# Moving a row scaling, table arithmetic, identity turns and activation-table loads in a whole-model kernel

## The chip, the cores and the metric

One core of a Trainium2 chip runs the whole program. The metric is the device time of one execution in microseconds (us); lower is better. The core has a matrix engine (PE), a vector engine (DVE), an activation engine (ACT), GpSimd (POOL) and a sync engine (SP) that issues transfers; each runs its own queue in order, and they meet only at semaphores.

## The reference

Two small networks run one after the other over 256 tokens of width 1024. The first also carries 256 context tokens. Its two layers are each a mixer (a gated delta rule, then attention), followed by an expert layer that picks 16 of 16384 experts per head and token. The second has two layers, each with a mixer, a feed-forward part with a causal convolution, and a gated embedding. What matters here:

```
def rmsnorm(x, gain):
    y = xf * lax.rsqrt(jnp.mean(xf * xf, axis=-1, keepdims=True) + EPS)
    return (y * gain).astype(x.dtype)

# the expert layer, per block of 128 tokens
    top_s, top_i = lax.top_k(s, PEER_TOPK)                 # 16 of 128, twice per head
    cand_s = top_s[..., 0, :, None] + top_s[..., 1, None, :]
    best_s, pos = lax.top_k(cand_s, PEER_TOPK)             # 16 of 256
    gate = jax.nn.softmax(best_s, axis=-1)
    act = jax.nn.gelu(jnp.einsum('pd,phkd->phk', xb, u_tab[idx]))
    return jnp.einsum('phk,phkd->pd', gate * act, v_tab[idx])

def conv_ffn(x, w_up, conv_w, conv_b, w_down):
    h = x @ w_up                                           # 1024 -> 5632
    hc = conv_b + sum(conv_w[j] * shifted(h, j) for j in range(3))
    g, up = jnp.split(hc, 2, axis=-1)
    return (jax.nn.silu(g) * up) @ w_down                  # 2816 -> 1024
```

The mixer of the second network's second layer is a state-space scan. It needs tables of powers of complex numbers (`Er`, `Ei`), which depend on weights alone and can be worked out at any time before it.

## The kernel before

The program is a list of stages (Begin, Ada, DeltaNet, Peer a, Attention, Peer m, FinalNorm, EvenMixer, Ffn 0, Ple 0, S5, Ffn 1, Ple 1, End). In a stage every engine has a hand-written order (`pe`, `dve`, `act`, `pool`, `sp`). Before its work in a stage an engine runs `enter`, which waits for all engines of the stage before; so no engine starts a stage until the last one has left the one before. Weights go through a ring of three 1 MB buffers that SP fills as PE frees them.

**Norms.** 128 tokens make a tile. ACT squares and sums one tile of a pair, DVE the other; DVE forms the mean, ACT takes the root (`Sqrt`, L340, L1618 or L2348), DVE inverts it (`reciprocal`) and scales the rows (`dve_scale`). PE turns the scaled tile in blocks of 128x128 into PSUM, and ACT and DVE each apply gain and shift to half of it while they copy it to `hT`. ACT evaluates functions from a table that must be loaded; the compiler puts a table load ahead of the first instruction that needs another one, so the one for the root stands between the squares and the root. While the first scaled tile is on its way, PE turns the identity 24 times into a bank that nobody reads (`pe_busy`, `BUSY = 24`). In the DeltaNet stage the first tile has already been scaled in the stage before.

**Expert stages (`Peer`).** Peer a has four tiles and 32 units (tile by head), Peer m two tiles and 16 units. For each unit `dve_choose` picks 16 experts: a generator with 14 steps, one or more DVE instructions each. POOL then gathers 16 rows of 8 KB per token, in 16 indirect transfers, into eight slots; DVE forms 16 dot products (`dve_dot`, L1993), ACT the gelu and a diagonal matrix, PE the weighted sum (L1858). A slot is filled again when PE has used it. The norm's scratch lies in the last two slots, so gather 6 waits until the last tile has passed the norm (`pool_rows`). Ahead of the sums, PE forms the queries and scores of eight half heads in pairs, jobs 0 to 7 (L1816, L1829): jobs 0 to 3, then the turns of tiles 2, 3 and 4, then jobs 4 to 7, for which all tiles must be in `hT`. The scaled rows have two buffers; in Peer a the fourth tile (number 3) needs the buffer of the second. DVE works through choice 0, choice 1, the scaling of tile 3, and then the units, with a step of the choice for the unit after next behind every dot product.

**Ffn 0.** The up projection is 44 chunks of 128 features (PE L300, four PSUM banks). For each chunk DVE does three instructions of the convolution (L2863, L2865, L2867) and, from chunk 22 on, a multiplication by the gate (L2872). Behind every chunk from the third on it also does two steps of the tables for the state-space mixer (L2745 to L2768); `pieces(c)` gives the number. The down projection (PE L262) starts when DVE has done chunk 43; DVE then adds its four results to the residual (L2879). Ffn 1 is the same without table steps.

Of the kernel before, what the change touches and what calls it, by code (L numbers as in the profile page):

```python
# [12 lines left out]
ACT = mybir.ActivationFunctionType  # L13
# [103 lines left out]
class Kit:  # L117


    def __init__(self, nc, ins, out, ctx):  # L120
# [13 lines left out]
        self.arena = self.tensor("arena", self.arena_n)  # L134
        self.top, self.rings = 0, [self.ring]

    def count(self, name, step=1):
# [7 lines left out]
    def tensor(self, name, n, dt=F32):  # L145
        return self.ctx.enter_context(self.nc.sbuf_tensor(name, [128, n], dt))[:, :]

    def al(self, n):
# [24 lines left out]
class Stage:  # L173
# [22 lines left out]
    def pe(self, e):  # L196
        pass
# [4 lines left out]
    def act(self, e):  # L202
        pass
# [105 lines left out]
class Norm:  # L309
# [88 lines left out]

    def pe(self, e):
        st = self.st  # L400
        self.pe_busy(e)
        for n in range(len(self.tiles)):
            e.wait_ge(*st.V.at(("n_x", n)))
            for half in range(2):
                if n >= 2:
                    e.wait_ge(*(st.V if half else st.S).at(("nT", n - 2)))
                for c in range(4):
                    m = st.turn(e, st.k.banks[(2 * n + half) % 4][:, c * 128:(c + 1) * 128],
                                self.xn[n % 2][:, (half * 4 + c) * 128:(half * 4 + c + 1) * 128])
                m.then_inc(*st.P.up(("nt", n, half)))  # L410
# [53 lines left out]
class Begin(Stage):  # L464
# [6 lines left out]
    def pool(self, e):  # L471
        k, i = self.k, self.k.i
        e.dma_start(k.cv, i["consts"][:, 0:k.nconst]).then_inc(*self.lc.up("c"))
        for name, d in (("ctx", 0), ("x", 2)):
            e.dma_start(k.X[:, d:d + 2, :], i[name][0].rearrange("(t p) d -> p t d", p=128)).then_inc(*self.lx.up())
# [108 lines left out]
class DeltaNet(Stage):  # L584
# [153 lines left out]
    def pe(self, e):  # L738
        k, P, ring = self.k, self.P, self.k.ring
        self.enter(e)  # L740
        self.norm.pe(e)
        e.wait_ge(*self.l_cw.at("l"))
# [941 lines left out]
class Peer(Stage):  # L1684
# [179 lines left out]
    def act(self, e):  # L1864
        k, P, V, S = self.k, self.P, self.V, self.S
        self.enter(e)
        self.norm.act_first(e)
# [12 lines left out]
        for u in range(self.units):  # L1880
            steps = self.act_steps(u)
# [72 lines left out]
    def dve(self, e):  # L1954
# [6 lines left out]
        for _ in self.dve_choose(e, 0):  # L1961
            pass
        for u in range(self.units):
            t = u // 8
            if u == 0:
                steps = itertools.chain(self.dve_choose(e, 1), self.dve_choose(e, 2))
                for _ in range(14):
                    next(steps)
                if self.nt > 2:
                    self.norm.dve_scale(e, 3)  # L1970
            else:
                steps = self.dve_choose(e, u + 2) if u + 2 < self.units else iter(())
# [9 lines left out]
            if u % 8 == 2 and u > 8:  # L1982
                self.dve_add(e, t - 1)
        self.dve_add(e, self.nt - 1)

    def dve_dot(self, e, u, s):
# [186 lines left out]
class Attention(Stage):  # L2173
# [76 lines left out]

    def act(self, e):
        self.enter(e)
        S = self.S
# [75 lines left out]
class FinalNorm(Stage):  # L2329
# [8 lines left out]

    def act(self, e):
        self.enter(e)  # L2340
        S = self.S
# [22 lines left out]
class EvenMixer(Stage):  # L2364
# [110 lines left out]

    def act(self, e):
        self.enter(e)
        S, V = self.S, self.V
# [293 lines left out]
class Ffn(Stage):  # L2772
# [35 lines left out]
    def pieces(self, c):  # L2808
        return 0 if self.l or c < 3 else 2

# [24 lines left out]
    def act(self, e):  # L2835
        k, V, S = self.k, self.V, self.S
        self.enter(e)
        self.norm.act(e)
# [11 lines left out]
    def dve(self, e):  # L2850
# [7 lines left out]
        for c in range(44):  # L2858
# [14 lines left out]
            for _ in range(self.pieces(c)):  # L2873
                next(steps, None)
        for n0 in (0, 512):
            for t in range(2):
# [5 lines left out]
class Ple(Stage):  # L2882
# [34 lines left out]
    def act(self, e):  # L2917
        S = self.S
        self.enter(e)
        self.norm.act(e)  # L2920
# [27 lines left out]
class S5(Stage):  # L2948
# [83 lines left out]
    def act(self, e):  # L3032
        V, S = self.V, self.S
        self.enter(e)
        self.norm.act(e)
# [178 lines left out]
```

## Time and profile before

| | |
|---|---|
| median of 3 runs | 4298.86 us (4298.03 to 4300.78) |
| profiled execution, its own time | 4287.95 us |
| its span in the trace | 4286.2 us |
| busy: PE, DVE, ACT, POOL | 85%, 59%, 23%, 28% |
| granted PE clock, mean | 0.966 of full |
| moved by the transfers | 1043.68 MB, mean 244 GB/s |

The span is the profiled execution from its first to its last instruction; the 1.75 us between it and the execution's own time lie around it. Stages in the trace, in us from the span's start: the first norm 36 to 48, the DeltaNet stage to 1115, Peer a 1115 to 2493, Attention to 2642, Peer m to 3350, Ffn 0 3517 to 3783, S5 from 3824, Ffn 1 4000 to 4240. A busy share is an average over all of them and says little of one place; what a change is worth there is read from the wait that ends last there.

### The profile page before, as it was taken

The numbers are of one execution on the slowest core, as the hardware profiler recorded it, in microseconds if no ns is written. First come the engines' busy times: TensorE is split into PE (matmuls) and PEld (weight loads), VectorE is DVE, ScalarE is ACT, GpSimd is POOL, SyncE is SP. The second block draws the span as 40 slices with busy tenths as digits, with TensorE's granted clock in tenths as the row PEclk, the third lists the DMA queues.
The fourth block names the chain that finished last, engine by engine and source line by source line (L and its number), as shares of the span: only waits on it lengthen the run. The fifth ranks groups of instructions, "written<-read, shape, count | busy, mean of one in ns | idle before, by whom it ended". The sixth has DMA issues, their size and how long they took to land.

```text
span 4286.2 us, 59878 instructions
## 1 busy us (share of the span) xinstructions
PE 3650.8 (85%) x23128; PEld 1996.2 (47%) x23128; DVE 2514.1 (59%) x5831; ACT 966.8 (23%) x2602; POOL 1219.4 (28%) x1257
## 2 busy tenths in 40 slices
PE   7988899888899977776777789887777889899999
PEld 3467544675444432222232236443222368555774
DVE  3466435564566777776777655667776348535341
ACT  2333113331222222222222213222222121010100
POOL 1054000440134444444444400344444010015000
PEclk9999999899999999999999999999999999999999
DMA  8200244001599999999999933999999334330443
GB/s 291 83 4 4 89 158 158 4 4 50 201 384 404 410 419 420 418 415 412 411 413 416 413 123 121 412 416 418 412 414 415 134 93 138 123 103 20 143 146 127
DMA packets 270115, 1043.68 MB, mean 244 GB/s; under 512 B 19931, under 2 KB 104166, under 8 KB 171530
## 3 DMA queue, kind: packets, MB, share of 16 engines
q0 software_dynamic: 115184, 815.62, 46.7%
q1 hardware_dynamic: 154650, 224.23, 15.5%
q8 instruction: 187, 3.06, 0.3%
q14 instruction: 94, 0.77, 0.1%
HBM read 1038.64 MB, written 1.13 MB: 243 GB/s over the span
## 4 chain that ended last, share of the span: by engine, by line
PE 52%; DMA 25%; DVE 12%; ACT 4%; issue 4%; POOL 3%; SPq 0%; DVEq 0%; POOLq 0%; ACTq 0%
DMA arena<-in_peer_uv,arena 25%; PE psum L262 13%; PE psum L1858 12%; PE psum L772 5%; PE psum L300 5%; PE psum L1816 4%; PE psum L816 3%; DVE arena L1993 2%; PE psum L213 2%; PE psum L1162 1%; POOL arena L1951 1%; PE psum L508 1%; ACT arena L1893 1%; PE psum L1173 1%; POOL arena L3055 1%
## 5 line engine op out<-in xcount | busy, mean ns | idle before, releaser
L1858 PE MATMUL psum<-arena 128*128 128x512 f32 x3072 | 1458.9, 620 | 394.1 <-ACT arena L1893 389.3
L1993 DVE SCALAR_TENSOR_TENSOR arena<-arena 128x1024 bf16<-128x1024 f32 x768 | 941.0, 1225 | 523.6 <-DMA arena<-in_peer_uv,arena 492.1
L1951 POOL DMA_INDIRECT arena<-in_peer_uv,arena x768 | 855.4, 1114 | 1184.8 <-PE psum L1858 1055.2
L1858 PEld LDWEIGHTS psum<-arena 128*128 128x128 f32 x3072 | 573.8, 195 | 1227.8 <-ACT arena L1893 634.6
L262 PE MATMUL psum<-ring,arena 128*128 128x512 f32 (+1 forms) x1344 | 576.4, 590 | 24.6 <-DVE arena L2872 9.1
L262 PEld LDWEIGHTS psum<-ring,arena 128*128 128x128 f32 x1344 | 254.2, 192 | 340.3 <-issue 315.1
L1886 ACT ACTIVATE arena<-arena 128x2 f32<-128x2 f32 x384 | 78.2, 204 | 1242.7 <-DVE arena L1993 1242.7
L1893 ACT ACTIVATE arena<-consts,arena 128x128 f32<-128x128 f32 x768 | 268.4, 394 | 224.0 <-DVE arena L2005 221.5
L300 PE MATMUL psum<-arena,ring 128*128 128x256 f32 x1408 | 309.6, 381 | 9.8 <-DVE arena L2867 7.7
L300 PEld LDWEIGHTS psum<-arena,ring 128*128 128x128 f32 x1408 | 267.0, 191 | 50.4 <-issue 6.4
L772 PE MATMUL psum<-arena,ring 128*128 128x512 f32 x512 | 229.0, 600 | 1.6 <-issue 1.6
L1816 PE MATMUL psum<-arena,ring 128*128 128x128 f32 (+3 forms) x704 | 183.0, 411 | 8.9 <-ACT arena L1631 8.9
L1816 PEld LDWEIGHTS psum<-arena,ring 128*128 128x128 f32 x704 | 120.7, 200 | 79.1 <-issue 50.8
L772 PEld LDWEIGHTS psum<-arena,ring 128*128 128x128 f32 x512 | 95.4, 191 | 127.4 <-issue 121.5
L213 PE MATMUL psum<-consts,arena 128*128 128x128 f32 (+3 forms) x706 | 102.9, 287 | 55.5 <-DVE arena L1672 12.3
L3055 POOL TENSOR_TENSOR arena<-arena 128x512 f32<-128x512 f32 x32 | 40.6, 1269 | 331.1 <-DVE arena L3090 331.1
L213 PEld LDWEIGHTS psum<-consts,arena 128*128 128x128 f32 (+3 forms) x706 | 84.0, 147 | 103.9 <-issue 44.6
L816 PE MATMUL psum<-ring,arena 128*128 128x512 f32 x256 | 110.4, 593 | 1.6 <-ACT arena L951 1.6
L2005 DVE SCALAR_TENSOR_TENSOR arena<-arena 128x2 f32<-128x2 f32 x384 | 80.9, 211 | 33.1 <-ACT arena L1886 31.4
L1014 DVE SCALAR_TENSOR_TENSOR arena<-arena 128x512 f32<-128x512 f32 x128 | 96.2, 752 | 4.5
L2863 DVE TENSOR_SCALAR arena<-psum,arena 128x256 f32<-128x256 f32 x88 | 47.6, 541 | 84.9 <-PE psum L300 84.7
L2879 DVE TENSOR_TENSOR x_res<-x_res,psum 128x512 f32<-128x512 f32 x8 | 5.5, 687 | 152.4 <-PE psum L262 152.4
(412 smaller groups left out, 3894.9 us busy)
## 6 DMA issues: line engine op xcount, KB each, us to landing
arena<-in_ada_w SPq DMA_DIRECT2D x48, 1024.0 KB, 7.1
ring<-in_ffn_w_up SPq DMA_DIRECT2D x44, 1024.0 KB, 5.0
ring<-in_dn_w_in SPq DMA_DIRECT2D x24, 1024.0 KB, 5.6
ring<-in_peer_w_query SPq DMA_DIRECT2D x22, 1024.0 KB, 7.0
ring<-in_ffn_w_down SPq DMA_DIRECT2D x20, 1024.0 KB, 5.0
arena<-in_peer_uv,arena POOLq DMA_INDIRECT x768, 12.8
ring<-in_ev_w_in SPq DMA_DIRECT2D x10, 1024.0 KB, 5.1
ring<-in_dn_w_out SPq DMA_DIRECT2D x8, 1024.0 KB, 4.8
```

The costliest lines, as they stand in the source:

```text
L213: return e.transpose(out, in_, self.k.const("ident")[0:n, 0:n])
L262: m = e.matmul(o, self.hT[:, k0 + k, t * 128:(t + 1) * 128], w[:, k, :], start=k0 + k == 0, stop=k0 + k == self.KC - 1)
L300: m = e.matmul(self.bank(c)[:, 0:self.nt], w[:, k, j * 128:(j + 1) * 128], self.hT[:, k, 0:self.nt], start=k == 0, stop=k == self.KC - 1)
L772: m = e.matmul(self.job_bank(j), w[:, q, j % 2 * 128:(j % 2 + 1) * 128], self.hT[:, q, :], start=q == 0, stop=q == 7)
L816: m = e.matmul(k.banks[t * 2 + nh], self.oT[:, k0 + q, t * 128:(t + 1) * 128], w[:, q, nh * 512:(nh + 1) * 512], start=k0 + q == 0, stop=k ...
L1014: e.scalar_tensor_tensor(acc, p[:, :, w:w + 256], self.cw[:, c, w:w + 1], acc, MUL, ADD).then_inc(*V.up(("conv", half, j)))
L1816: m = e.matmul(k.banks[j % 2][:, 0:w_], w[:, n, c % 2 * 128:(c % 2 + 1) * 128], self.hT[:, n, a * 128:b * 128], start=n == 0, stop=n == 7)
L1858: m = e.matmul(k.banks[4 + t % 2 * 2 + nh], self.diag[g % self.ND], self.vsl[g % self.NS][:, nh * 512:(nh + 1) * 512], start=u % 8 == 0 an ...
L1893: e.activation(self.diag[g % self.ND], k.const("ident"), ACT.Copy, bias=0.0, scale=self.cf[u % 2][:, s:s + 1]).then_inc(*S.up(("dg", g)))
L1951: e.indirect_dma_start(self.uv[g % self.NS], None, self.table(), bass.IndirectOffsetOnAxis(ap=self.eid[u % 6][:, s:s + 1], axis=0)).then_i ...
L1993: e.scalar_tensor_tensor(self.junk[g % 2], self.us[g % self.NS], 1.0, self.h[:, u // 8, :], MUL, MUL, accum_out=self.a[u % 2][:, s:s + 1]) ...
L3055: e.tensor_tensor(self.xr[i % 8], self.w2[i % 4], self.two(T.Er[:, i, :]), MUL).then_inc(*G.up())
```

## The change

- The 24 identity turns are left out in the norm of the DeltaNet stage; the other norms keep them.
- `root_table` is called first thing by ACT in ten stages, ahead of `enter`: a `Sqrt` of one column that POOL has set to 1 at the start of the program. The table load moves to it.
- In Peer a DVE scales tile 3 between choice 0 and choice 1.
- In both expert stages choice 2 starts behind the third dot product of unit 0 and not behind the first (`late`).
- In Ffn 0 DVE does two table steps behind chunks 3 to 21 and one behind chunks 22 to 43, and the rest behind chunk 43, while PE is in the down projection.

```diff
+    def root_table(self, e):
+        e.activation(self.warm[1], self.warm[0], ACT.Sqrt, bias=0.0, scale=1.0)
...
-    def pe(self, e):
+    def pe(self, e, busy=True):
         st = self.st
-        self.pe_busy(e)
+        if busy:
+            self.pe_busy(e)
...
     def pool(self, e):
         k, i = self.k, self.k.i
+        e.memset(k.warm[0], 1.0).then_inc(*self.G.up())
...
-        self.norm.pe(e)
+        self.norm.pe(e, busy=False)
...
     def act(self, e):
         k, P, V, S = self.k, self.P, self.V, self.S
+        k.root_table(e)
         self.enter(e)
...
         for _ in self.dve_choose(e, 0):
             pass
+        if self.nt > 2:
+            self.norm.dve_scale(e, 3)
+        for _ in self.dve_choose(e, 1):
+            pass
         for u in range(self.units):
             t = u // 8
             if u == 0:
-                steps = itertools.chain(self.dve_choose(e, 1), self.dve_choose(e, 2))
-                for _ in range(14):
-                    next(steps)
-                if self.nt > 2:
-                    self.norm.dve_scale(e, 3)
+                steps = self.late(self.dve_choose(e, 2), 2)
...
+    def late(self, steps, n):
+        for _ in range(n):
+            yield
+        yield from steps
...
     def pieces(self, c):
-        return 0 if self.l or c < 3 else 2
+        return 0 if self.l or c < 3 else 2 if c < 22 else 1
...
+        for _ in steps:
+            pass
         for n0 in (0, 512):
```

**Order of DVE in Peer a, where choice 0 ends.** The 128x16 SCALAR_TENSOR_TENSOR ends a choice, `x_res,arena 128x1024` is the scaling of a tile, and 128x1024 SCALAR_TENSOR_TENSOR a dot product. Before (the rest of choice 1 is left out):

```order
L2073 SCALAR_TENSOR_TENSOR arena<-arena 128x16
L2024 MAX arena<-arena 128x8
...
L2073 SCALAR_TENSOR_TENSOR arena<-arena 128x16
L1672 TENSOR_SCALAR arena<-x_res,arena 128x1024
L1993 SCALAR_TENSOR_TENSOR arena<-arena 128x1024
L2024 MAX arena<-arena 128x8
L2026 MAX_INDEX arena<-arena 128x8
L1993 SCALAR_TENSOR_TENSOR arena<-arena 128x1024
L2028 MATCH_REPLACE arena<-arena 128x128
L2030 MAX arena<-arena 128x8
L2002 RECIPROCAL arena<-arena 128x1
```

The same place in the changed kernel:

```order
L2087 SCALAR_TENSOR_TENSOR arena<-arena 128x16
L1679 TENSOR_SCALAR arena<-x_res,arena 128x1024
L2038 MAX arena<-arena 128x8
...
L2087 SCALAR_TENSOR_TENSOR arena<-arena 128x16
L2007 SCALAR_TENSOR_TENSOR arena<-arena 128x1024 x2
L2016 RECIPROCAL arena<-arena 128x1
L2019 SCALAR_TENSOR_TENSOR arena<-arena 128x2
L2007 SCALAR_TENSOR_TENSOR arena<-arena 128x1024
L2038 MAX arena<-arena 128x8
L2040 MAX_INDEX arena<-arena 128x8
```

The scaling has moved ahead of choice 1, and the first steps of choice 2 behind the third dot product.

**Order of DVE in Ffn 0, at its end.** The first four rows of a chunk are the convolution and the gate (128x256 to 128x254), 128x1016 and 128x8x127 are table steps, `x_res` is the residual. Before:

```order
L2872 TENSOR_TENSOR arena<-arena 128x256
L2764 TENSOR_TENSOR arena<-arena 128x1016
L2768 TENSOR_TENSOR arena<-arena 128x8x127
L2863 TENSOR_SCALAR arena<-psum,arena 128x256
L2865 SCALAR_TENSOR_TENSOR arena<-psum,arena 128x255
L2867 SCALAR_TENSOR_TENSOR arena<-psum,arena 128x254
L2872 TENSOR_TENSOR arena<-arena 128x256
...
L2879 TENSOR_TENSOR x_res<-x_res,psum 128x512 x4
```

In the changed kernel:

```order
L2785 TENSOR_TENSOR arena<-arena 128x8x127
L2882 TENSOR_SCALAR arena<-psum,arena 128x256
L2884 SCALAR_TENSOR_TENSOR arena<-psum,arena 128x255
L2886 SCALAR_TENSOR_TENSOR arena<-psum,arena 128x254
L2891 TENSOR_TENSOR arena<-arena 128x256
L2778 TENSOR_TENSOR arena<-arena 128x1016
L2781 TENSOR_TENSOR arena<-arena 128x1016
L2785 TENSOR_TENSOR arena<-arena 128x8x127
...
L2900 TENSOR_TENSOR x_res<-x_res,psum 128x512 x4
```

Fifteen table steps now stand behind the last chunk and ahead of the four additions.

**Order of ACT where Ffn 0 begins.** `x_res 128x1024` is the square, 128x2 the root. Before:

```order
L451 ACTIVATE arena<-psum 128x4x128 x2
L335 ACTIVATE arena<-x_res 128x1024
L340 ACT_TABLE_LOAD
L340 ACTIVATE arena<-arena 128x2
L348 ACTIVATE arena<-psum,vc 128x128 x8
```

In the changed kernel:

```order
L457 ACTIVATE arena<-psum 128x4x128 x2
L151 ACT_TABLE_LOAD
L151 ACTIVATE warm<-warm 128x1
L340 ACTIVATE arena<-x_res 128x1024
L345 ACTIVATE arena<-arena 128x2
L353 ACTIVATE arena<-psum,vc 128x128 x8
```

The load has moved ahead of the wait for the stage before and of the square; there are as many loads as before. On PE the only difference is that the one row of 24 identity turns ahead of DeltaNet's first tile is gone; SP's order is the same.

## Rows read from the trace of the kernel before

**Rows 1.** The page, chain that ended last: share of the span by engine.
```profile
PE 52%; DMA 25%; DVE 12%; ACT 4%; issue 4%; POOL 3%; SPq 0%; DVEq 0%; POOLq 0%; ACTq 0%
```

**Rows 2.** Timeline, first norm: start, length, engine, line, operation, out<-in [idle before <-releaser].
```profile
36.15 4.48 PE L213 MATMUL psum<-consts 128*128 128x128 f32 x24 [0.81 <-PE psum L562]
...
38.54 0.60 POOL L722 DMA_DIRECT2D arena<-in_dn_conv_w  x1
...
41.54 1.36 DVE L385 TENSOR_SCALAR arena<-psum,mod 128x128 f32<-128x128 f32 x4 [3.85 <-PE psum L213]
...
48.16 3.65 PE L754 MATMUL psum<-arena,ring 128*64 128x512 f32 x16 [1.08 <-ACT arena L348]
```

**Rows 3.** One line's answer, L722: its transfer.
```profile
DMA to landing us min/median/max: 5.6/5.6/5.6
```

**Rows 4.** Windows, first norm: length, busy PE, PEld, DVE, ACT, POOL, clock, DMA, GB/s.
```profile
36.15:40.40 4.25, 4.25 (x24) 4.25 (x25) 1.54 (x1) 0.00 (x0) 3.95 (x8) 0.60 1.05 384
...
40.40:48.10 7.70, 4.58 (x40) 3.83 (x37) 6.56 (x19) 6.24 (x17) 4.25 (x8) 1.00 1.05 350
```

**Rows 5.** Timeline, first expert stage, before its sums.
```profile
1134.07 5.68 ACT L1631 ACTIVATE arena<-psum,mod 128x128 f32<-128x128 f32 x16
...
1136.03 0.17 DVE L2073 SCALAR_TENSOR_TENSOR arena<-arena 128x16 uint32<-128x16 f32 x1
...
1145.55 0.74 DVE L1672 TENSOR_SCALAR arena<-x_res,arena 128x1024 f32<-128x1024 f32 x1
...
1147.57 2.90 ACT L1631 ACTIVATE arena<-psum,mod 128x128 f32<-128x128 f32 x8 [7.81 <-PE psum L213]
...
1150.52 6.45 PE L1816 MATMUL psum<-arena,ring 128*128 128x128 f32 x32 [2.14 <-ACT arena L1631]
```

**Rows 6.** Windows, the same stage: cold stretch, first sums, later sums.
```profile
1146.40:1156.00 9.60, 7.42 (x33) 7.05 (x34) 1.03 (x2) 3.18 (x9) 1.89 (x2) 0.50 1.01 423
...
1167.00:1203.00 36.00, 36.00 (x94) 16.78 (x93) 24.49 (x64) 8.45 (x25) 13.65 (x12) 0.96 0.82 296
...
1500.00:1900.00 400.00, 306.79 (x651) 121.27 (x651) 296.34 (x747) 100.44 (x279) 174.98 (x160) 0.97 1.01 418
```

**Rows 7.** Timeline of DVE, feed-forward 0, two table steps in a chunk.
```profile
3616.84 0.54 DVE L2863 TENSOR_SCALAR arena<-psum,arena 128x256 f32<-128x256 f32 x1
...
3618.86 1.20 DVE L2764 TENSOR_TENSOR arena<-arena 128x1008 f32<-128x1008 f32 x1
...
3621.22 0.54 DVE L2863 TENSOR_SCALAR arena<-psum,arena 128x256 f32<-128x256 f32 x1
...
3742.49 0.69 DVE L2879 TENSOR_TENSOR x_res<-x_res,psum 128x512 f32<-128x512 f32 x1 [39.41 <-PE psum L262]
```

**Rows 8.** Timeline of PE, feed-forward 0.
```profile
3587.79 56.28 PE L300 MATMUL psum<-arena,ring 128*128 128x256 f32 x260
...
3644.49 3.69 PE L300 MATMUL psum<-arena,ring 128*128 128x256 f32 x16 [0.42 <-DVE arena L2867]
...
3703.18 7.09 PE L262 MATMUL psum<-ring,arena 128*128 128x512 f32 x9 [6.96 <-DVE arena L2872]
```

**Rows 9.** Timeline of PE, feed-forward 1, where the down projection starts.
```profile
4161.80 4.94 PE L262 MATMUL psum<-ring,arena 128*128 128x512 f32 x7 [2.18 <-DVE arena L2872]
```

**Rows 10.** Windows, start of both down projections.
```profile
3703.20:3709.20 6.00, 6.00 (x7) 2.48 (x8) 0.00 (x0) 0.00 (x0) 0.00 (x0) 0.50 0.00 0
...
4161.80:4166.60 4.80, 4.80 (x8) 2.02 (x9) 0.00 (x0) 0.00 (x0) 0.00 (x0) 0.64 0.46 180
```

**Rows 11.** Groups by line, table loads of L340: busy us, mean ns, idle.
```profile
L340 ACT ACT_TABLE_LOAD x7 | 9.0, 1283 | 0.1
```

**Rows 12.** Timelines of three norms: first turns on data.
```profile
2498.44 1.97 PE L213 MATMUL psum<-consts,arena 128*128 128x128 f32 x16 [0.49 <-DVE arena L392]
...
3520.59 2.34 PE L213 MATMUL psum<-consts,arena 128*128 128x128 f32 x20 [0.88 <-DVE arena L392]
...
3828.78 1.91 PE L213 MATMUL psum<-consts,arena 128*128 128x128 f32 x16
```

More of the change, by code:

```diff
@@ L135, in __init__ @@
         self.top, self.rings = 0, [self.ring]
+        self.warm = [self.tensor(f"warm{n}", 1) for n in range(2)]
     def count(self, name, step=1):
@@ L2251, in act @@
     def act(self, e):
+        self.k.root_table(e)
         self.enter(e)
@@ L2339, in act @@
     def act(self, e):
+        self.k.root_table(e)
         self.enter(e)
@@ L2476, in act @@
     def act(self, e):
+        self.k.root_table(e)
         self.enter(e)
@@ L2836, in act @@
         k, V, S = self.k, self.V, self.S
+        k.root_table(e)
         self.enter(e)
@@ L2918, in act @@
         S = self.S
+        self.k.root_table(e)
         self.enter(e)
@@ L3033, in act @@
         V, S = self.V, self.S
+        self.k.root_table(e)
         self.enter(e)
```

## The prediction

> **What bounds the kernel now.** I read the page's chain first, then the chain in order of time, to find which stages are held by what; then the timeline at each place the change touches, and windows for clock and transfers. The chain is more than half PE, a quarter transfers and an eighth DVE [rows 1], but no edit touches the bulk of any of these: each sits at a seam, where one engine waits for another. The reader should look, at each seam, for the idle time ahead of the instruction that leads on. There are four kinds.
>
> In the first norm PE turns 24 identities, 4.48 us, while nobody else works, and only then the data on which DVE waits 3.85 us [rows 2]. In Peer a ACT is done with tiles 1 and 2 at 1139.75 and idles until tile 3 arrives at 1147.57, because DVE ran all of choice 1 ahead of that tile's scaling [rows 5]. In Ffn 0 PE gets through a chunk (16 matmuls) each 56.28 x 16 / 260 = 3.46 us until 3644, and is then held by DVE chunk for chunk [rows 8]; DVE takes 4.38 us for a chunk with two table steps [rows 7]. In the other norms PE waits for the scaled rows 0.49 or 0.88 us, or not at all [rows 12]. The measurement of this kernel can tell some 0.2%, 8.6 us, from no change.
>
> **Ffn 0, the largest term.** One table step is taken from each chunk from 22 on. A chunk's own work on DVE is 3618.86 - 3616.84 = 2.02 us, a step 1.20 [rows 7]: 3.22 per chunk, under PE's 3.46. PE finished chunk 31 at 3644.07 (the 56.28 us piece), so chunk 22 at 3644.07 - 9 x 3.46 = 3612.9; DVE came to it at 3616.84, 3.9 us late. It gains 0.24 per chunk, is level with PE near chunk 38, and meanwhile stays far inside the four banks. So PE is never held, and ends chunk 43 at 3644.07 + 12 x 3.46 = 3685.6. Ffn 1 is the model for what follows: there, without table steps, PE waits 2.18 us for the last chunk [rows 9]. The down projection then starts at 3687.8 and not at 3703.18 [rows 8]: 15.4 us. If DVE does not catch up (22 chunks of 3.3 from 3616.84) it is 13.8.
>
> The 15 steps left over, 15 x 1.20 = 18 us, are hidden by the down projection: the first addition to the residual comes 39.3 us after the projection starts [rows 7, 8]. Without that cover they would cost 18 us.
>
> The wait before the down projection also left PE at half clock: 0.50 over the first 6.00 us of it, which is 3.0 us lost; Ffn 1, after its short wait, ran 4.80 us at a mean of 0.64, so 72% of it at half, 1.7 lost [rows 10]. I take Ffn 1's case, 1.3 us more; at best 3.0. Term: **16.7 us**, 13.8 to 18.4.
>
> **Peer a, tile 3.** Choice 0 ends at 1136.2, and the buffer that the scaling needs is free (ACT already copies that tile from 1134.07). The scaling, 0.74, ends near 1137.0 and not at 1146.3. PE turns it at once, but ACT is on tiles 1 and 2 until 1139.75; then come its 2.90 us for tile 3, and jobs 4 to 7 can start at 1142.7 where they started at 1150.52 [rows 5]: 7.8 us. What is late next is ACT, not DVE: choice 1 ends 0.7 later, at 1146.2, while the first gelu needs jobs 4 to 7 to be done; two of them took 6.45 us [rows 5], so all four end near 1153. Gathers 6 and 7, behind the norm on POOL, move with it. Then the clock: PE ran at half from 1146.4 to 1156.0 [rows 6], so 5.5 us of these jobs, 2.7 lost. PE's idle time is now broken by the eight turns, so part of that may return; zero to 2.7, and I take 1.0, nearer to zero because the rest of the idle stretch remains. From the first sums on, everything hangs on the slots that PE frees; the transfers have room there (0.82 busy) and are full only later (1.01) [rows 6], so the whole full stretch starts earlier with the same bytes. Term: **8.8 us**, 7.8 to 10.5.
>
> **First norm.** The eight turns of tile 0 start at 36.15; at the pace of the identity turns, 4.48 / 24 = 0.187, they end at 37.65, and DVE's copy begins 3.9 us earlier than 41.54 [rows 2]. Not all of this arrives. The five turns of the convolution weights stand in PE's queue ahead of the gate matmuls, and these weights land at 38.54 + 5.6 = 44.1 whatever PE does [rows 2, 3]; with up to 0.9 for the turns, the matmuls start near 44.9 and not 48.16: 3.3 us. Against it stands the clock: over the identity turns it was 0.60 on average, and 1.00 over the stretch behind them [rows 4]. With the gaps that real turns have, the half level may last into the matmuls, and each us of it there costs 0.5. None gives 3.3; lasting to 50.5 gives 0.5. I take 2 us of it: **2.3 us**.
>
> The Trainium skill, TensorE: Matmul & The Clock Gate, part 4 (PE-mode transpose), says that turns do not count as PE activity as matmuls do and that the full clock does not engage for them. By that rule the 24 turns never raised the clock, leaving them out costs nothing, and this term would be 3.3, the sum 31.1. The trace disagrees: PE had nothing but these turns from 36.15, and the clock was full behind them [rows 4]. I go by the trace.
>
> **Square root's table.** A load is 1.28 us [rows 11] and stood behind the square. Where it moves ahead of `enter`, ACT was waiting for the stage before. What it frees is capped by PE's idle time before its first turns on data [rows 12]: 0.49 in Attention, 0.88 in Ffn 0 and (the same row) in Ffn 1. In S5 PE goes straight from the identity turns to the data, so nothing; the same holds in both expert stages, the two Ple stages load it while PE is in another projection, FinalNorm waits for its gain row, and EvenMixer has the table already. Behind these caps the identity turns are late next. Term: **2.3 us**; 1.5 if the small root itself delays `enter` where ACT had worked until just before.
>
> **Choice 2 later; POOL's memset.** Two of 14 choice steps move from a stretch in which DVE waits into the sums of unit 0. The nearest row for a step is the table step, 1.20, so at most 2.4 per stage if nothing hid it; but DVE is busy 24.49 of 36.00 us in the first sums [rows 6]. I take 0, bounds -0.5 to +1.2. The memset, one column ahead of the first loads on POOL, is 0 to 0.1.
>
> **Sum.** 16.7 + 8.8 + 2.3 + 2.3 = 30.1 us. Against the profiled execution's own 4287.95 (span 4286.2 and 1.75 around it) that is 4257.9. This execution was 10.9 faster than the median of the runs shown, so for a median I predict 4298.86 - 30.1 = **4268.8 us**. With all low ends the gain is 22, with all high ends 35: 4264 to 4277.
>
> **Rivals.**
> - *The gathers swallow Peer a's gain.* For it: the transfers are full for most of the stage, and gathers 0 to 5 start no earlier. Against it: only eight slots exist, so the early start of six moves nothing behind them, and the transfers have room in the first sums. The gain would be 21.3: 4277.6.
> - *The table steps were not what held PE*, so Ffn 0 stays as it was and the change does not do there what it says. Against it: PE's waits name DVE's L2867 [rows 8], and Ffn 1, with the same loads and chunks, has none of them. The gain would be 13.4: 4285.5.
> - *Slower: PE stays at half clock without the identity turns*, through the gate matmuls and DeltaNet's first projections, which PE sets. Every us at half costs 0.5, so it decides from 60 us at half clock on. At 90 us it costs 45, and with the other terms kept the time is 4298.86 - 30.1 + 45 = 4313.8. For it: the half level lasted 9.6 us at one place with PE 77% busy [rows 6]. Against it: 90 us is nine times that, and these matmuls follow without gaps.
>
> **Chances.** Forecast 0.73, gathers 0.12, Ffn 0 unchanged 0.06, half clock 0.04, and 0.05 for small terms adding up beyond the high end. The range reaches from a little under the high end, for the spread between executions (the profiled one and the median are 10.9 apart), to past the first rival: 4257 to 4281; the forecast alone 4264 to 4277. Faster by over 0.2% holds for the forecast, the first rival, two thirds of the second and what lies beyond the high end: 0.94. Within 0.2% are the rest of the second, where another term fails too, and a mild half clock: 0.03. Slower: 0.03.
>
> **What would show it.** In the changed profile, Ffn 0: no idle PE between chunks, about 2.2 us of it before the down projection, and 15 table steps beside that. Peer a: jobs 4 to 7 start about 3 us after ACT is through with tile 2, not 10.8. First norm: the gate matmuls start about 8.8 us after the first turn of the stage, not 12.0. Norms of Ffn 0 and 1: no PE idle before the turns. It is wrong if in Ffn 0 the down projection starts over 50 us after chunk 32 (before 58.7, forecast 43.3), or if Peer a from its first sum to its last grows by what its start gained.

## Result and the profile after the change

| | before | after |
|---|---|---|
| median of the runs, us | 4298.44 (4296.43 to 4300.78, 4 runs) | 4259.48 (4256.97 to 4262.81, 4 runs) |
| profiled execution, own time (span), us | 4287.95 (4286.2) | 4262.81 (4261.0) |
| mean granted clock | 0.966 | 0.969 |

The ratio is 0.991, 95% interval 0.9892 to 0.9927. The change makes the kernel faster by 39.0 us between medians; forecast were 30.1, a time of 4268.8 and a range of 4257 to 4281. The time lies in the range, but 4.5 us below the fast end of the forecast alone (4264 to 4277). The interval in us is 31 to 46. In a second measurement (e8 below) the gain was 35.9 us, interval 0.9904 to 0.9931, which is 29.6 to 41.2 us. So the gain is probably some us more than the sum of 30.1: the first interval excludes it, the second does not. The two profiled executions differ by only 25.1 us, because that of before was a quick one (4287.95, where 29 later runs of the same kernel had a median of 4294.77) and that of after was the slowest of its four.

The page of after, the chain that ended last by engine, answers to [rows 1]: DVE has lost 3 points of it.

```profile
PE 54%; DMA 26%; DVE 9%; ACT 4%; issue 3%; POOL 2%; DVEq 0%; POOLq 0%; ACTq 0%
```

**Ffn 0.** PE's timeline of after. The columns here and below: start, length, engine, line, operation, operands, count, and in brackets the idle time before it and who ended it.

```profile
3567.82 110.67 PE L305 MATMUL psum<-arena,ring 128*128 128x256 f32 x512
3680.67 9.68 PE L267 MATMUL psum<-ring,arena 128*128 128x512 f32 x22 [2.18 <-DVE arena L2891]
```

The 512 matmuls of the last 32 chunks are now one row without a wait: 110.67 / 32 = 3.46 us a chunk, the pace that the prediction took from [rows 8]. Chunk 32 starts at 3567.82 + 20 x 3.46 = 3637.0, so the down projection starts 43.7 us after it (before 58.7, forecast 43.3), behind the 2.18 us that [rows 9] had promised. DVE's timeline shows where the table steps went:

```profile
3680.60 1.22 DVE L2778 TENSOR_TENSOR arena<-arena 128x1016 f32<-128x1016 f32 x1
...
3697.49 1.22 DVE L2785 TENSOR_TENSOR arena<-arena 128x1016 f32<-128x1016 f32 x1
...
3716.99 0.69 DVE L2900 TENSOR_TENSOR x_res<-x_res,psum 128x512 f32<-128x512 f32 x1 [18.28 <-PE psum L267]
```

From 3680.60 to 3697.49 there are fifteen of them, all beside the down projection, and DVE then still waits 18.28 us for the first sum. Nothing of them is on the path.

**Peer a.** The timeline of the seam that [rows 5] shows for before:

```profile
1137.17 8.47 ACT L1638 ACTIVATE arena<-psum,mod 128x128 f32<-128x128 f32 x24
...
1139.22 0.74 DVE L1679 TENSOR_SCALAR arena<-x_res,arena 128x1024 f32<-128x1024 f32 x1
...
1140.11 1.97 PE L218 MATMUL psum<-consts,arena 128*128 128x128 f32 x8 [2.84 <-ACT arena L1638]
...
1145.69 5.91 PE L1823 MATMUL psum<-arena,ring 128*128 128x128 f32 x32 [3.62 <-ACT arena L1638]
```

ACT's idle time of 7.81 us is gone: its 16 copies for tiles 1 and 2 and the 8 for tile 3 are one row of 24. ACT is late next, as forecast. It is through with tile 2 after 16 / 24 of 8.47, at 1142.82, and jobs 4 to 7 start 2.9 us later (before 10.8, forecast 3). The window of 9.6 us from these jobs on, which answers to the first of [rows 6]:

```profile
1145.60:1155.20 9.60, 9.36 (x62) 9.17 (x63) 5.91 (x16) 1.38 (x6) 3.28 (x4) 0.77 1.00 414
```

The clock is 0.77 there, where it was 0.50.

**First norm.** Timeline of after, against [rows 2], and the windows against [rows 4] (length, busy PE, PEld, DVE, ACT, POOL, clock, DMA, GB/s):

```profile
37.06 3.41 PE L218 MATMUL psum<-consts,arena 128*128 128x128 f32 x16 [0.82 <-PE psum L569]
...
38.80 1.36 DVE L390 TENSOR_SCALAR arena<-psum,mod 128x128 f32<-128x128 f32 x4 [0.66 <-PE psum L218]
...
40.01 0.94 POOL L729 DMA_DIRECT2D arena<-in_dn_conv_w  x1
...
46.02 0.49 PE L218 MATMUL psum<-consts,arena 32*128 32x32 f32 x5 [2.11 <-DMA arena<-in_dn_conv_w]
...
46.44 5.35 PE L761 MATMUL psum<-arena,ring 128*64 128x512 f32 x16
```

```profile
40.40:46.40 6.00, 2.64 (x22) 2.10 (x21) 5.15 (x15) 5.06 (x12) 5.95 (x11) 0.97 1.06 357
46.40:51.80 5.40, 5.40 (x19) 1.54 (x18) 0.32 (x1) 0.23 (x1) 0.00 (x0) 0.68 0.36 121
```

The gate matmuls follow the stage's first turn by 9.4 us (before 12.0, forecast 8.8). PE was held by the convolution weights, as expected, which POOL issued 1.5 us later than in [rows 2]: 0.9 because the stage itself began later, and 0.5 because the second of the two memsets ahead of them took 1.07 us and not 0.53. It took about 1.07 in all the other traces with it ahead of the weights (e1 to e9, e11, e12), so this is not an effect of the change, and the trace of before was the lucky one. The start won 1.7 us, and the same 16 matmuls took 5.35 us at a clock of 0.68 where they had taken 3.65: 1.7 lost. The first projection begins at 51.72 (before 51.74). By these two traces alone, the first norm gave nothing.

**Norm of Ffn 0**, against [rows 12]: the turns on data follow the identity turns at once.

```profile
3510.78 2.81 PE L218 MATMUL psum<-consts 128*128 128x128 f32 x24 [0.83 <-PE psum L267]
3513.57 1.97 PE L218 MATMUL psum<-consts,arena 128*128 128x128 f32 x16
```

### The profile page after: what moved, and what is told of

It reads as the page before. It is cut to its first block, busy times and chain, and to the rows that moved or that the text cites. A ratio compares the mean times of both kernels' runs of the same rounds, so it can differ in the third digit from the quotient of the medians.

```text
span 4261.0 us, 59845 instructions
## 1 busy us (share of the span) xinstructions
PE 3639.4 (85%) x23104; PEld 1989.0 (47%) x23104; DVE 2517.2 (59%) x5831; ACT 968.8 (23%) x2612; POOL 1221.6 (29%) x1258
## 3 DMA queue, kind: packets, MB, share of 16 engines
q1 hardware_dynamic: 154650, 224.23, 15.7%
## 4 chain that ended last, share of the span: by engine, by line
PE 54%; DMA 26%; DVE 9%; ACT 4%; issue 3%; POOL 2%; DVEq 0%; POOLq 0%; ACTq 0%
DMA arena<-in_peer_uv,arena 26%; PE psum L267 13%; PE psum L1865 12%; PE psum L305 7%; PE psum L779 5%; PE psum L1823 3%; PE psum L823 3%; DVE arena L2007 2%; PE psum L218 2%; PE psum L1169 1%; ACT arena L1901 1%; PE psum L1180 1%; PE psum L515 1%; POOL arena L3078 1%; POOL arena L1959 1%
## 5 line engine op out<-in xcount | busy, mean ns | idle before, releaser
L1415 POOL COPY arena<-arena 32x128 f32<-32x128 f32 x128 | 38.1, 297 | 174.3 <-DVE arena L1540 166.3
```

## Experiments

Gains are given between medians against the kernel before on the same chip; an interval in us is that of the ratio times 4295. Since every kernel's trace has the same matmuls, identity turns apart, stretches between the starts of the same matmul can also be compared in 14 traces (before, after, e1 to e12), and the table below holds them. The stretch of Peer a starts at the turns of tile 2, 15.5 us into the stage in every trace; the last three rows start at the stage's first identity turn. E10 is not in the first row, since it has a second edit there. One trace stands for each kernel (two for the whole change). By "pattern of the clock" I mean at which seams the granted clock is full and at which it is half. Within one pattern the late stretches repeat within 0.2 us, which no run of the whole program does.

| stretch, by PE's starts | traces without the edit, us | traces with it, us | gain |
|---|---|---|---|
| first matmul to DeltaNet's second half | 514.3 to 517.7, mean 515.8 (9) | 511.0 to 514.0, mean 512.4 (4) | 3.4 |
| Peer a | 1358.8 to 1362.5, mean 1360.5 (8) | 1350.8 to 1353.5, mean 1352.1 (6) | 8.5 |
| Ffn 0 and Ple 0: table steps | 307.57 to 307.65 (5) | 290.77 (e1) | 16.8 |
| the same, root's table on top | 290.77 (e1) | 288.17 to 288.21 (5) | 2.6 |
| S5: root's table | 175.87 or 175.88 (6) | 174.39 to 174.41 (5), or 177.41 and 177.58 (2) | 1.5, or -1.6 |
| Ffn 1 and Ple 1: root's table | 278.67 or 278.68 (5) | 276.06 or 276.07 (4), or 277.50 to 277.55 (3) | 2.6, or 1.1 |

### e1: the table steps of Ffn 0 alone

```diff
-        return 0 if self.l or c < 3 else 2
+        return 0 if self.l or c < 3 else 2 if c < 22 else 1
...
+        for _ in steps:
+            pass
```

> Only Ffn 0's table steps are moved; everything else is as in the kernel before. My theory (DVE's second table step per chunk held PE from chunk 32 on): the down projection of Ffn 0 starts 43 to 45 us after chunk 32 (58.7 before), and the time falls by 16.7 us (13.8 to 18.4). Rival theory, that the 9 us by which the medians moved more than my sum sit here (the steps beside the down projection or the chunks gave more than counted): 22 us or more. Second rival, that the table steps did not hold PE: 0 to -2 us.

Measured: 4277.46 us, ratio 0.9965, interval 0.9951 to 0.9979, so 9 to 21 us; medians 18.3. PE's timeline of this kernel, where [rows 8] had a wait per chunk and 6.96 us before the down projection:

```profile
3599.78 87.36 PE L300 MATMUL psum<-arena,ring 128*128 128x256 f32 x404
3689.32 10.95 PE L262 MATMUL psum<-ring,arena 128*128 128x512 f32 x21 [2.18 <-DVE arena L2872]
```

The stretch is 16.8 us shorter than in every trace without the edit. That is the term (16.7). The time alone (9 to 21) excludes both rivals, 22 or more and none.

### e2: Peer a's order alone

```diff
+        if self.nt > 2:
+            self.norm.dve_scale(e, 3)
+        for _ in self.dve_choose(e, 1):
+            pass
...
-                steps = itertools.chain(self.dve_choose(e, 1), self.dve_choose(e, 2))
-                for _ in range(14):
-                    next(steps)
-                if self.nt > 2:
-                    self.norm.dve_scale(e, 3)
+                steps = self.late(self.dve_choose(e, 2), 2)
```

> Only Peer a's order on DVE is changed (tile 3 scaled after choice 0, choice 2 two steps late). My theory: jobs 4 to 7 start 7.8 us earlier against the start of the stage, the gain is kept to the end, and the time falls by 8.8 us (7.8 to 10.5). Rival theory (the gathers swallow it): the gain at the end of the stage is 0 to 2 us. Third theory, for the 9 us that the medians moved beyond my sum: an earlier start frees the transfers also later, and the time falls by 14 us or more.

Measured: 4288.25 us, ratio 0.9982, interval 0.9973 to 0.9991 (4 to 12 us); medians 7.5. The stretch of Peer a took 1352.95 us in this trace; the mean of the six traces with the edit is 8.5 under that of the eight without. It is all won before the sums: from the stage's start to the first sum it takes 39.0 to 39.8 us in the six (mean 39.4) and 47.2 to 48.5 in the eight (mean 48.2), and from the first sum to the last a mean of 1324.6 against 1324.3. So the gathers neither swallow the gain nor add to it, and the third theory falls.

### e3: the first norm without identity turns, alone

```diff
-        self.norm.pe(e)
+        self.norm.pe(e, busy=False)
```

> Only the 24 identity turns of the first norm are left out. The sum's term: 2.3 us less (0.5 to 3.3). What the trace of the changed kernel suggests instead: the gate matmuls start 1.7 us earlier and run 1.7 us longer at half clock, so 0 us, with the end of those matmuls level with the kernel before. By the rule that turns do not count for the clock, the matmuls would take the same 3.65 us and the gain would be 3.3.

Measured: 4294.97 us, ratio 0.9994, interval 0.9985 to 1.0003 (-1 to 6 us); medians 0.8. All three answers lie in that interval, so the time decides nothing; e9 asks again. The trace decides one thing: from the start of the gate matmuls to that of the first projection it takes 5.28 us, as in both traces of the whole change, and 3.58 in every trace with the turns. The answer in which they take the same 3.65 is wrong here. In e12, which has the same edit, they took 3.58.

### e4: square root's table alone

The memset that feeds the small root is in it too.

```diff
+    def root_table(self, e):
+        e.activation(self.warm[1], self.warm[0], ACT.Sqrt, bias=0.0, scale=1.0)
...
+        k.root_table(e)
         self.enter(e)
```

> Only the loads of square root's table ahead of the stages' waits, and the memset that feeds them, are added. My term: 2.3 us less (1.5 to 2.3), all of it in the norms of Attention (0.49), Ffn 0 (0.88) and Ffn 1 (0.88), where PE no longer idles before its first turns on data. Rival, for the 9 us that the medians moved beyond my sum: the loads free more stages than these, 6 us or more. Other rival: the small root delays ACT at the seams, and the time does not fall or rises by 1 us.

Measured: 4288.69 us, ratio 0.998, interval 0.9971 to 0.9989 (5 to 12 us); medians 7.1. My 2.3 lies outside. The trace, norm of Ffn 0, beside [rows 12]:

```profile
3523.85 2.81 PE L218 MATMUL psum<-consts 128*128 128x128 f32 x24 [0.83 <-PE psum L267]
3526.64 1.97 PE L218 MATMUL psum<-consts,arena 128*128 128x128 f32 x16
```

The gap that I had counted is gone. But the last three stretches are 2.1, 1.5 and 2.6 us shorter, 6.2 together, which is more than the gaps in them (0.88 twice). The rest is time at half clock that no longer occurs: 1.5 in S5, whose 24 identity turns took 2.81 us and not 4.48, and 1.2 and 1.7 in the first matmuls of the two down projections. The next two kernels split the edit.

### e5 and e6: the table ahead in three stages, and in the others

```diff
 # e5: only in Attention and the two Ffn; e6: only in Peer, FinalNorm, EvenMixer, Ple and S5
+        k.root_table(e)
```

> Square root's table is loaded ahead only in Attention, Ffn 0 and Ffn 1 (and the memset is there); the loads ahead in both expert stages, FinalNorm, EvenMixer, the two Ple stages and S5 are left out. The loads in all ten stages together gave 7.1 us between medians, where my term was 2.3. My theory, that only these three norms gain: as much as all ten together, 7 us, or 2.3 if the rest of the 7.1 is not the table's. Rival, that stages which I cost at nothing gain too: 2 to 3 us here, and the rest in the next kernel.

> The opposite half: square root's table is loaded ahead in both expert stages, FinalNorm, EvenMixer, the two Ple stages and S5, and not in Attention and the two Ffn stages. My theory: 0 us. Rival: 4 to 5 us less.

Measured: e5 4291.43 us, ratio 0.9992 (0.9982 to 1.0001), medians 3.3; e6 4296.09 us, ratio 1.0001 (0.9992 to 1.0009), medians -1.3. By the times alone the rest gives nothing (-4 to 3 us), as my theory said, but what the three norms give is not told from nothing either (-0.4 to 8). The halves sum to 2.0, the whole had given 7.1. The traces say why they need not add. In e5 Ffn 0's stretch is 2.1 us shorter, S5's 1.1 longer (it has no edit there) and Ffn 1's 1.1 shorter, 2.1 in all. In e6, which left Ffn 0's and Ffn 1's norms alone, the three are 1.3, 1.5 and 1.7 shorter, 4.5 in all, and EvenMixer, which took 156.8 to 160.3 us in the other thirteen traces, took 165.1. That last one has a wait behind it: DVE's two row scalings in its norm took 5.71 us, and PE waited 2.52 us for the second. DVE's timeline in e6, then in e7, where PE did not wait:

```profile
3368.03 5.71 DVE L397 TENSOR_SCALAR arena<-x_res,arena 128x1024 f32<-128x1024 f32 x2
```

```profile
3363.82 2.19 DVE L397 TENSOR_SCALAR arena<-x_res,arena 128x1024 f32<-128x1024 f32 x2
```

Why they took so long in this one trace is open. The others come without a longer wait; e9 shows one bare.

S5 in e5 shows what the term had missed. PE's timeline, to be read against the last of [rows 12]:

```profile
3831.26 2.81 PE L218 MATMUL psum<-consts 128*128 128x128 f32 x24 [2.19 <-DVE x_res L2961]
3834.95 1.97 PE L218 MATMUL psum<-consts,arena 128*128 128x128 f32 x16 [0.88 <-DVE arena L397]
```

This stage has no edit in e5. Its identity turns ran at full clock, and behind them stands the same gap of 0.88 us as in the Ffn stages. In the trace of before they took 4.48 us at half clock and covered it:

```profile
3824.47 4.48 PE L213 MATMUL psum<-consts 128*128 128x128 f32 x24 [2.19 <-DVE x_res L2945]
```

### e7: the memset alone

```diff
+        e.memset(k.warm[0], 1.0).then_inc(*self.G.up())
```

> Only the memset of one column ahead of POOL's first loads is added, with its two small buffers; no table load is moved. My theory: 0 us (0 to 0.1 slower). Rival, that the start of the loads or the changed layout of the code makes part of the gain of the fourth edit: 3 to 7 us less. If it is 0, this run says how far two kernels with the same work lie apart in a measurement, and gives a second trace of the stages as they were before.

Measured: 4295.86 us, ratio 0.9999 (0.999 to 1.0008): no effect, medians 1.1 apart, which is also how far equal work lies apart here.

### e8: the whole change again

The kernel after the change, unedited, in a longer measurement.

> The whole change once more, in more runs and beside the parts. The four parts alone gave 18.3, 7.5, 0.8 and 7.1 us between medians, 33.7 in all; the first comparison of the whole change gave 39.0 from four runs of each. If the parts add up: 31 to 36 us. If they help each other: 39 or more. My sum before was 30.1.

Measured: 4258.91 us, ratio 0.9917 (0.9904 to 0.9931), medians 35.9. The four parts alone had summed to 33.7: they add up within what can be measured (each part's interval is 8 to 12 us wide).

### e9: the whole change, identity turns kept

```diff
-        self.norm.pe(e, busy=False)
+        self.norm.pe(e)
```

> The whole change, but with the 24 identity turns of the first norm kept. Beside the whole change (35.9 us under the kernel before) this says what their removal is worth in it. By my term: 2.3 us less gain, so 33.6. By the first norm of the traces alone, where a start 1.7 us earlier was given back in matmuls at half clock: 0, so 35.9. By the time from PE's first instruction to the second half of DeltaNet, which is 511.0 and 511.7 us in the two traces of the whole change and 514.3 to 517.7 in seven traces with the turns: 3 to 4, so 32 to 33; the trace of this run would then show 515 or more there.

Measured: 4265.71 us, ratio 0.9931 (0.9917 to 0.9944), medians 31.3 under before, against 35.9 and 39.0 for the whole change. The stretch to DeltaNet's second half is 515.5 us, as the third answer had it. That is 4.6 or 7.7 us for the edit (e3 had given 0.8), with intervals that overlap; the traces' means give 3.4, and I go by them. Counted from the stage's first turn, which leaves out what came before it, the two groups lie closer together: 487.3 to 489.5 us in the nine traces with the turns, 484.8 to 485.5 in the four without. The 0 that I had read from the first norm of one pair of traces does not hold for the stretch.

This trace shows something else. S5 is the same program in e8 and e9. PE's timeline in e8, then in e9, then the windows of 16 us from the first identity turn:

```profile
3794.28 4.48 PE L218 MATMUL psum<-consts 128*128 128x128 f32 x24 [2.19 <-DVE x_res L2967]
3798.60 1.91 PE L218 MATMUL psum<-consts,arena 128*128 128x128 f32 x16
...
3804.58 1.06 PE L3034 MATMUL psum<-arena,consts 128*128 128x256 f32 x2 [1.44 <-DVE arena L3096]
```

```profile
3799.22 2.81 PE L218 MATMUL psum<-consts 128*128 128x128 f32 x24 [2.19 <-DVE x_res L2967]
3802.01 1.97 PE L218 MATMUL psum<-consts,arena 128*128 128x128 f32 x16
...
3808.05 0.67 PE L3034 MATMUL psum<-arena,consts 128*128 128x256 f32 x2 [1.44 <-DVE arena L3096]
```

```profile
3794.28:3810.28 16.00, 13.09 (x76) 11.28 (x78) 10.86 (x24) 5.94 (x14) 0.59 (x1) 0.79 0.15 59
```

```profile
3799.22:3815.22 16.00, 13.09 (x92) 10.94 (x93) 13.75 (x29) 5.94 (x14) 3.58 (x3) 1.00 0.15 58
```

The waits are the same to 0.01 us, and the same work stands in front. Only the clock differs: the 24 turns take 4.48 us or 2.81, and the matmuls behind them 1.06 or 0.67 a pair. S5 takes 177.58 or 174.39 us by that, Ffn 1 277.55 or 276.06.

### e10: fewer turns where they are late, and the weights first

```diff
+        self.norm.BUSY = 16      # EvenMixer, S5; Ffn: 24 if l == 0 else 16
...
+        e.dma_start(self.cr[0:32, :]... i["dn_conv_w"]...)
         for b in self.gb:
             e.memset(b, 0.0).then_inc(*G.up())
```

> The whole change, with 16 identity turns and not 24 in the norms of EvenMixer, S5 and Ffn 1, and with POOL issuing the convolution weights of DeltaNet ahead of its two memsets. Theory (the identity turns are late next): in the trace of the whole change they end 1.6 to 1.9 us after the scaled rows are there in these three norms, so 1.5 us each, and the weights' wait in the first norm goes, 1.1: about 5.6 us under the whole change. Rival (the clock): with fewer turns PE stays at half clock into the turns on data and beyond, and the gain is 0 to 2 us.

Measured: 4255.58 us, ratio 0.991 (0.9896 to 0.9923), medians 41.5 under before. Its gain is the largest of all, and 5.6 us under the whole change was expected, but its interval (33 to 45 us) overlaps both of the whole change (31 to 46 and 29.6 to 41.2); that it beats it is not shown. In the trace the weights' edit does what it should: they no longer hold PE, and the gate matmuls take 3.65 us again:

```profile
45.35 3.65 PE L761 MATMUL psum<-arena,ring 128*64 128x512 f32 x16 [1.00 <-ACT arena L353]
48.93 0.70 PE L779 MATMUL psum<-arena,ring 128*128 128x512 f32 x1
```

From PE's first matmul to the first projection it takes 38.6 us; the whole change took 41.5 twice and 40.2 in e12, kernels with the turns 41.7 to 44.9. To DeltaNet's second half it took 508.0 us, against 511.0 to 514.0 in the first row of the table. EvenMixer took 156.8 us, where twelve traces with 24 turns (all but e6) took 158.6 to 160.3; this is one trace, but the term of 1.5 that I had counted there may well be real. The fewer turns gave nothing in S5 and Ffn 1: 174.41 and 276.06 us, as with 24 in e9. PE waits 0.85 us for the data instead:

```profile
3796.17 1.94 PE L218 MATMUL psum<-consts 128*128 128x128 f32 x16 [2.18 <-DVE x_res L2969]
...
3798.95 1.97 PE L218 MATMUL psum<-consts,arena 128*128 128x128 f32 x16 [0.85 <-DVE arena L397]
```

That the turns were 1.6 us late in S5 and Ffn 1 in the whole change came from their half clock, not from their number.

### e11: identity turns in a wait

```diff
         self.up.pe(e, between)
+        if self.l:
+            for _ in range(12):
+                self.turn(e, k.banks[7][:, 256:384], k.const("ident"))
         e.wait_ge(*V.at(("c", 43)))
```

> The kernel before, with 12 identity turns put into the 2.18 us for which PE waits ahead of Ffn 1's down projection. Its stretch from the start of Ffn 1's identity turns to PE's last matmul was 278.67 us in every trace in which neither that norm nor the last stage was changed, and the first 4.80 us of the down projection ran at a mean clock of 0.64. If turns hold the clock as matmuls do: 1.00 there and 277.0 us. If they do not count: 0.64 and 278.7. If they outlast the wait, a few tenths more than either.

It ran only once, and its time of 4290.34 us is no measure of 1.7 us. PE's timeline, and the window that answers to the second of [rows 10]:

```profile
4163.52 1.47 PE L213 MATMUL psum<-consts 128*128 128x128 f32 x12
4165.86 10.54 PE L262 MATMUL psum<-ring,arena 128*128 128x512 f32 x24 [0.87 <-DVE arena L2875]
```

```profile
4165.86:4170.66 4.80, 4.80 (x11) 2.17 (x12) 0.00 (x0) 0.00 (x0) 0.00 (x0) 1.00 0.50 195
```

The wait still ends when DVE is done, but the projection behind it now runs at 1.00 where it had run at 0.64, and the stretch is 276.97 us and not 278.67 or 278.68 as in five other traces. Up to this wait the trace is like those five (S5 took 175.87 us, and the down projection starts 161.45 us into the stage), so beside them the turns made the difference.

They were not needed in every kernel, though. In the eight other traces (after, e4, e5, e6, e8, e9, e10, e12) the same window ran at 1.00 behind the same wait of 2.18 us with no turn in it. E6 is the closest: its down projection too starts 161.45 us into the stage, and its stretch is 276.98 us. What differs lies in the stages ahead of it (S5 took 174.41 us):

```profile
4173.27 7.11 PE L267 MATMUL psum<-ring,arena 128*128 128x512 f32 x16 [2.18 <-DVE arena L2889]
```

```profile
4173.27:4178.07 4.80, 4.80 (x12) 2.17 (x13) 0.00 (x0) 0.00 (x0) 0.00 (x0) 1.00 0.48 185
```

So one trace speaks for the turns, and the same 1.7 us also came by another pattern of the clock alone. The Trainium skill, TensorE: Matmul & The Clock Gate, part 4 (PE-mode transpose), says that turns do not count as PE activity as matmuls do and that the full clock does not engage for them; by that rule this window would have stayed at 0.64. This trace speaks against it, and so do [rows 2] and [rows 4], where the clock rose while PE did nothing but turns.

### e12: choice 2 without its delay

```diff
-                steps = self.late(self.dve_choose(e, 2), 2)
+                steps = self.late(self.dve_choose(e, 2), 0)
```

> The whole change, but in both expert stages choice 2 starts with the first step of unit 0 again and not two steps late. My theory: the delay is worth 0 (the whole change without it is between 0.5 us slower and 1.2 us faster), and the expert stage's stretch in the trace is that of the whole change, 1351 to 1353 us. Rival, that the delay is part of Peer a's gain: 2 us or more slower, and 1354 us or more there. The stretches of S5 and Ffn 1, which this leaves as they are, say on what the clock's pattern depends: 177.5 and 277.5 us in both traces of the whole change, 174.4 and 276.1 with the first norm's identity turns kept. If the pattern is the program's own, it stays at 177.5; if any change ahead can tip it, either pair may come.

Measured: 4255.88 us, ratio 0.9908 (0.9893 to 0.9922), medians 38.7 under before; the stretch of Peer a took 1350.8 us, against 1351.1 to 1353.5 in the five with the delay. The delay is worth nothing that these runs can see. S5 and Ffn 1 took 174.39 and 276.07 us, where both traces of the whole change took 177.4 to 177.6 and 277.5. The edit lies over 1000 us ahead of S5 and changes no wait there. Whether it tipped them, or the single execution did, one trace cannot say.

## Why the prediction was right, and where it was not

- **Ffn 0, 16.7 us: right.** 16.8 in the stretch that differs only by this edit. The leftover steps are hidden, and DVE still waits 18.28 us behind them. Of the parts, e1's trace has the down projection 13.9 us earlier than before in a stage that began 1.6 later, so 15.5 (counted 15.4); the other 1.3 is clock, as counted.
- **Peer a, 8.8 us: right.** 8.5 in the traces' means, 7.5 between medians (4 to 12). Of the parts, jobs 4 to 7 start 7.9 us earlier in the stage (25.9 us after its first turn, before 33.8; counted 7.8), and the first sum 8.8 us earlier in the means, so 0.9 is clock (counted 1.0). The rival on the gathers falls: from the first sum to the last the time is the same, 1324.6 us against 1324.3.
- **First norm, 2.3 us: near in size, by luck.** The stretch to DeltaNet's second half is 3.4 us shorter in the means of 9 and 4 traces, but only 1.1 of it is won in the norm. Counted from the stage's first turn, the first projection starts after 15.7 us with the identity turns (mean of nine) and after 14.7, 15.2, 15.3 and 13.0 without. The start gained what the weights' landing left, and the half clock took most of it back in three traces and not in the fourth, e12. "Full clock: 3.3; lasting to 50.5: 0.5" was about the right pair of bounds (2.7 and 0.4 to 1.0 measured), but three of four lie at the low one and I had taken 2.3. The other 2.3 us come between the first projection and DeltaNet's second half, where nothing was edited; no run shows from what.
- **Square root's table, 2.3 us: the term that was mis-sized.** The gaps in front of the first turns were counted right (0.49, 0.88, 0.88; they are gone). "In S5 nothing" was read from a trace in which the identity turns there ran at half clock and so hid the wait; at full clock a gap of 0.88 us stands there (e5), and with the load moved it is gone (e4, e9). The seams also move the clock: the last three stretches together gave 6.2 us with this edit alone, 2.1 in e5; on top of e1's, they gave 2.6 - 1.6 + 1.1 = 2.1 in both traces of the whole change and 2.6 + 1.5 + 2.6 = 6.7 in e9, e10 and e12. In Ffn 0 the 2.6 on top of e1's are 0.9 of gap and 1.7 of clock: the first 6 us of the down projection ran at 0.72 in e1 and at 1.00 in after. With Attention's 0.5 (its first turns on data start 4.4 us into the stage in all seven traces with the edit, 5.0 in the others) the term is 2.6 or 7.2 us, by the clock's pattern; the times of e4 (5 to 12) fit the second, those of e5 the first.
- **Choice 2's delay and the memset, 0: nothing else is seen** (e12, e7), within intervals of some us.
- **Sum.** 16.8 + 8.5 + 3.4 + 2.6 = 31.3, or 35.9 with the better pattern. Forecast were 30.1, measured 39.0 and 35.9. If the unprofiled runs mostly have the better pattern, nothing is missing; if they have that of the two profiled ones, 5 to 8 us are unexplained, at the edge of the intervals. This is open: of an unprofiled run the record has the mean clock (0.969 to 0.970 in the four after the change), but not the seams at which it fell.
- **Rivals.** Gathers: fell (e2). Table steps not what held PE: fell (e1). Half clock without identity turns: its mechanism is seen, 1.7 us over the gate matmuls in three of four traces, but the half level lasted a few us and not the 60 from which it decides.

## What to carry to other kernels

Where an engine that others wait for (here DVE) does two jobs in turn, compare its time per round with that of the engine behind it: 4.38 against 3.46 us a round cost 16.8 us, and moving what nobody waits for behind the loop won it back whole. A seam's gain is its gap, plus or minus what the matmuls behind it run at: take both clock levels as bounds, and do not judge a seam of 2 us by one pair of traces. A gap of nothing in front of the data can be a gap hidden by slow identity turns: ask what would wait if they ran at full clock. Filling a short wait in front of long matmuls with turns of a constant is worth trying, if they end before the wait does; here one trace speaks for it.

## What the runs showed of the hardware

- With turns of a constant in a wait of 2.18 us the granted clock of the matmuls behind it was 1.00 (e11), where it was 0.64 or 0.65 without them in the five traces that are like it up to there: 1.70 us. In eight other traces it was 1.00 without them (e6: 276.98 us against e11's 276.97).
- The same 24 identity turns took 2.81 us at full clock and 4.48 at half (S5 in e9 and e8). The slower ones hid a wait of 0.88 us for the data (S5 in e5).
- The granted clock behind the same wait (2.19 us) and the same work differed between two kernels that differ only 3700 us earlier: 0.79 and 1.00 over 16 us, 3.2 us of time (e8, e9). S5 took one of four lengths in 14 traces (174.4, 175.9, 177.0, 177.5 us), each within 0.2 us; of the seven traces without an edit in it six took 175.9, and e5 177.0. What tips it, the kernel or the single execution, stays open.
- The same program's times spread over 20 us (4285.28 to 4304.85 in 29 runs of before), while stretches of 300 us repeated to 0.1 us in five traces (307.57 to 307.65). Of the stages, DeltaNet spreads most in the traces (1080.6 to 1086.5 us in the nine with the first norm's turns); Peer a, Attention and Peer m spread by about 3 us each.
